# Output projection in eight pieces on the key tiles, MLP operands in pairs, chunk one split early: a two-layer fp32 encoder step on one core

## The reference, cut to what matters

```python
x = x + o.reshape(bsz, t, H * 64) @ w_o          # output projection, 1024 x 1024
x = x + sq_relu_mlp(rmsnorm(x, norm_ffn[l]), w_up[l], w_down[l])   # 1024 -> 4096 -> 1024

def sq_relu_mlp(h, w_up, w_down):
    return jnp.square(jax.nn.relu(h @ w_up)) @ w_down
```

## Time and profile before

| | us |
|---|---|
| median of three runs | 1664.33 (1663.49 to 1667.38) |
| the profiled execution's own time | 1654.25 |
| its span, first to last instruction | 1652.4 |
| PE busy | 1533.6 |
| DVE busy | 1108.5 |
| ACT busy | 728.2 |
| POOL busy | 431.2 |
| mean granted TensorE clock, share of full | 0.970 |

### The profile page before, as it was taken

How to read it: one execution, slowest core, us unless ns; L and a number is a source line. 1 busy time by engine, 2 the same in 40 slices (tenths; PEclk the granted TensorE clock), 3 DMA queues, 4 the chain that set the end, 5 groups by cost and what they waited for, 6 DMA issues and landing times.

```text
span 1652.4 us, 30854 instructions
## 1 busy us (share of the span) xinstructions
PE 1533.6 (93%) x10826; PEld 1445.4 (87%) x10826; DVE 1108.5 (67%) x1970; ACT 728.2 (44%) x1500; POOL 431.2 (26%) x441
## 2 busy tenths in 40 slices
PE   4999979998979999999999897999897999999997
PEld 3787759997969999999988686998886999999997
DVE  4132037775788788788765236778478888888875
ACT  3313137774444433333334434777444334333424
POOL 1110034552342122122100003455243221222210
PEclk8999969999989999999999998999999999999999
DMA  7245331211021221331240537221022123312211
GB/s 261 87 141 159 125 98 49 58 40 52 26 77 52 102 102 51 102 102 51 76 144 11 180 135 220 65 64 33 1 77 77 63 90 102 102 53 99 102 51 58
DMA packets 119316, 146.06 MB, mean 88 GB/s; under 512 B 17632, under 2 KB 95520, under 8 KB 119248
## 3 DMA queue, kind: packets, MB, share of 16 engines
q1 hardware_dynamic: 119248, 145.16, 26.9%
HBM read 120.54 MB, written 24.60 MB: 88 GB/s over the span
## 4 chain that ended last, share of the span: by engine, by line
PE 80%; issue 6%; DVE 5%; ACT 4%; DMA 2%; POOL 1%; SPq 1%; POOLq 0%; DVEq 0%; ACTq 0%
PE ps L1663 47%; PE ps L1990 19%; PE ps L1825 3%; PE ps L1869 2%; PE ps L1870 2%; PE ps L1871 2%; ACT wh L861 1%; DVE wl L1204 1%; PE ps L1840 1%; PE ps L1796 1%; PE ps L1848 1%; POOL sacc L712 1%; PE ps L1818 1%; DVE wul L1406 0%; ACT wuh L1010 0%
## 5 line engine op out<-in xcount | busy, mean ns | idle before, releaser
L1496 DVE TENSOR_TENSOR xT<-xT,ps 128x592 f32<-128x592 f32 (+1 forms) x256 | 194.9, 762 | 51.3 <-PE ps L1663 49.0
L812 POOL TENSOR_TENSOR ssum<-raw 128x512 f32<-128x512 f32 x32 | 42.9, 1341 | 485.3 <-DVE wul L1406 482.2
L1990 PE MATMUL ps<-bh,wuh 128*128 128x296 f32 (+1 forms) x512 | 153.3, 299 | 11.3 <-issue 4.4
L744 POOL TENSOR_TENSOR prob<-prob,rs 128x144 f32<-128x144 f32 (+4 forms) x160 | 117.0, 745 | 140.4 <-DVE rs L1310 140.2
L1990 PE MATMUL ps<-bl,wuh 128*128 128x296 f32 (+1 forms) x512 | 153.2, 299 | 0.0
L1990 PE MATMUL ps<-bh,wul 128*128 128x296 f32 (+1 forms) x512 | 152.7, 298 | 0.0
L1320 DVE TENSOR_TENSOR ptl<-ps,pth 128x256 fp32r<-128x256 f32 (+2 forms) x192 | 95.9, 502 | 65.3 <-ACT pth L948 65.2
L1663 PE MATMUL ps<-wh,xgh 128*128 128x512 f32 (+5 forms) x320 | 122.8, 384 | 11.5 <-issue 4.3
L1990 PE MATMUL ps<-th,wuh 128*128 128x296 f32 (+1 forms) x384 | 116.2, 303 | 13.5 <-DVE snap L1476 11.0
L1663 PE MATMUL ps<-wl,xgh 128*128 128x512 f32 (+5 forms) x320 | 121.9, 381 | 0.0
L1663 PE MATMUL ps<-wh,xgl 128*128 128x512 f32 (+5 forms) x320 | 121.5, 380 | 0.0
(11 more groups left out here) (244 smaller groups left out, 4674.0 us busy)
## 6 DMA issues: line engine op xcount, KB each, us to landing
raw<-in_w_up SPq DMA_DIRECT2D x32, 1024.0 KB, 7.1
raw<-in_w_down SPq DMA_DIRECT2D x32, 1024.0 KB, 5.1
raw<-in_w_in_a SPq DMA_DIRECT2D x12, 1024.0 KB, 7.3
kv_mla<-stn SPq DMA_DIRECT2D x24, 256.0 KB, 2.4
raw<-in_w_o_a SPq DMA_DIRECT2D x4, 1024.0 KB, 7.2
natk<-kv_mla SPq DMA_DIRECT2D x8, 512.0 KB, 3.5
raw<-in_w_o_b SPq DMA_DIRECT2D x4, 1024.0 KB, 12.1
q_mla<-stn SPq DMA_DIRECT2D x16, 192.0 KB, 1.9
```

The source lines that it names most:

```text
L744: g.tensor_tensor(prob[0:rows, c, off:off + n], prob[0:rows, c, off:off + n], rs[0:rows, u:u + 1].to_broadcast([rows, n]), ALU.mult).then_ ...
L812: g.tensor_tensor(ssum[:, 1, :, :], a11, a21, ALU.subtract).then_inc(s_ready, 1)
L1496: v.tensor_tensor(a, a, two_banks(2 + m % 2, n), ALU.add).then_inc(x_ready if last else acc_done, 1)
L1990: i = te.matmul(ps[:, bank, 0:h], w[:, k, :], x, start=(u not in (3, 4, 6) and k == 0 and p == 0), stop=(k == 3 and p == 2), skip_group_ch ...
```

## The change

- w_o comes in eight pieces of 128 columns (0.5 MB each, 512-byte runs), all issued by `load_wo`, in layer 0 ahead of block 5's stores, in layer 1 where the four were. `wo_high` and `wo_low` split a piece into one of two places in turn, which are those of the keys (`kh`, `kl`) of the even and the odd heads. Piece 0 is split inside head 15's step, piece 1 behind the last turned group and ahead of `out(15)`, piece m+2 in step m of `operands`. To make that possible, `prob`, `kh`, `kl`, `qh`, `ql`, `pth` and `ptl` get new places, and the memsets of `prob` are ten for five.
- PE begins piece 0 between the last attention products: k-steps 0 and 1 ahead of head 15's first weighted product, 2 to 6 behind the last turn, and 7 behind `out(15)` (`wo_first`).
- MLP operands: B21 with B22 and T2 with T3 are made by one instruction each on ACT and DVE; the sign of B12 is turned with a negated gain (`gN`) so that T2 and T3 are one broadcast sum; T4 gets a place of its own.
- POOL's weight sums of chunk 0 stand one by one behind the sums of squares of steps 2 to 5, those of chunk 1 behind those of steps 6 and 7. Chunk 0's units are split in steps 2, 4, 5, 6 (three) and 7, where it was four in step 6 and three in 7.
- First period: ACT splits chunk 1's units 2 to 6 ahead of the inner squares; DVE splits units 2 and 3 between the combinations, takes the variance later, and copies the spread and does both norms behind the last combination.
- The raw slots of the MLP change (up 0 and 2, sums in 1, down 3), with the waits of the first loads; the load of q_down's first half no longer waits for the last down split.

```diff
-W_IN0, WO_A0 = 0, 12
-KVD0, QD0, KVU0, QU0, WO_B0, W_END = 16, 18, 20, 22, 26, 30
+KVD0, QD0, KVU0, QU0, W_END = 12, 14, 16, 18, 22
...
+        def wo_raw(m):
+            return raw[:, m // 2, 1024 * (m % 2):1024 * (m % 2) + 1024].rearrange("p (k c) -> p k c", c=P)
+        def wo_half(t, m):
+            return t[:, 4 + 2 * (m % 2):6 + 2 * (m % 2), :].rearrange("p u (k c) -> p (u k) c", c=P)
...
+            def load_wo(layer):
+                sp.wait_ge(lo_done, KVD0 if layer == 0 else W_END)
+                for m in range(KD):
+                    sp.dma_start(wo_raw(m), wo_src(layer, m)).then_inc(wo_in, 16)
...
             for b, (kind, hf) in enumerate(BLOCKS):
-                for j in (2 * b + 4, 2 * b + 5):
-                    load(j)
+                if b < 4:
+                    for j in (2 * b + 4, 2 * b + 5):
+                        load(j)
+                if b == 5:
+                    load_wo(0)
...
             load(KVD0 + 1)
+            load(QD0)
             sp.wait_ge(dl_done, 4 * NCH)
-            load(QD0)
...
+            def wo_high(layer, m):
+                act.wait_ge(wo_in, 128 * (layer + 1))
+                if m == 0:
+                    act.wait_ge(s_ps, 5 * (HEADS * layer + HEADS - 1))
+                elif m == 1:
+                    act.wait_ge(s_ps, 5 * HEADS * (layer + 1))
+                else:
+                    act.wait_ge(wo_ps, KD * layer + m - 1)
+                s.activation(wo_half(wuh, m), wo_raw(m), ACT.Copy).then_inc(wo_hi, 1)
...
                         exp(h, c, u)
+                        if last and u == 0:
+                            wo_high(layer, 0)
...
+                wo_high(layer, 1)
                 out(HEADS - 1, 1, PAIRS - 1)
...
+            def wo_low(layer, m):
+                dve.wait_ge(wo_in, 128 * (layer + 1))
+                dve.wait_ge(wo_hi, KD * layer + m + 1)
+                v.tensor_tensor(wo_half(wul, m), wo_raw(m), wo_half(wuh, m).bitcast(F32), ALU.subtract).then_inc(wo_lo, 1)
...
                     if not last:
                         qk(h, 2, 1 - c)
+                    else:
+                        wo_low(layer, 0)
                     row_max(h, 3)
...
+                    dve.wait_ge(wo_ps, KD * layer + m + 1)
                     a = halves(xT[:, m, 0:n])
                     v.tensor_tensor(a, a, two_banks(m % 2, n), ALU.add).then_inc(x_ready, 1)
+                    if m + 2 < KD:
+                        wo_low(layer, m + 2)
...
-                        scaled(t24[:, 0:h], m, second, t1f[:, k, 0:h], ALU.add)
-                        scaled(t3f[:, 0:h], m, second, b12[:, k, 0:h], ALU.subtract)
-                        lo_x("B21", k, m, first)
-                        lo_x("B22", k, m, second)
-                        lo_tmp("T2", k, t24[:, 0:h])
-                        scaled(t24[:, 0:h], m, first, t24[:, 0:h], ALU.subtract)
-                        lo_tmp("T3", k, t3f[:, 0:h])
-                        lo_tmp("T4", k, t24[:, 0:h])
+                        x22 = xT[:, m, second].unsqueeze(1).to_broadcast([P, 2, h])
+                        v.scalar_tensor_tensor(t23[:, :, 0:h], x22, gain_of(m), pre[k][:, :, 0:h],
+                                               ALU.mult, ALU.add).then_inc(op_tmp, 1)
+                        hi_ready("B21", k)
+                        v.scalar_tensor_tensor(operand_pair("B21", k, True, h), halves(xT[:, m, 0:2 * h]), gain_of(m),
+                                               operand_pair("B21", k, False, h).bitcast(F32), ALU.mult, ALU.subtract).then_inc(op_lo, 1)
+                        tmp_ready("T2", k)
+                        hi_ready("T2", k)
+                        v.tensor_tensor(operand_pair("T2", k, True, h), t23[:, :, 0:h],
+                                        operand_pair("T2", k, False, h).bitcast(F32), ALU.subtract).then_inc(op_lo, 1)
...
+                for m in range(KD):
+                    step(m, {2: (0,), 4: (1,), 5: (2,), 6: (3, 4, 5), 7: (6,)}.get(m, ()))
...
-                    if not down:
-                        variance(b - 1, 6)
                     dve.wait_ge(p_ps, c * 7 + (7 * c0 + 7 + 5))
                     combine(c, snap[:, 2, 0:h], 1, snap[:, 0, 0:h], ALU.add)
                     dve.wait_ge(u_add, c * 5 + (5 * c0 + 5 + 2))
                     combine(c, hu[:, 1, h:n], 2, snap[:, 2, 0:h], ALU.subtract)
+                    if not down:
+                        variance(b - 1, 6)
                     dve.wait_ge(p_ps, c * 7 + (7 * c0 + 7 + 6))
                     combine(c, hu[:, 1, 0:h], 3, snap[:, 2, 0:h], ALU.add)
+                    if down:
+                        norm(c + 1, 1)
+                    else:
+                        up_lo(layer, c + 2, par, 2, True)
+                    dve.wait_ge(p_ps, c * 7 + (7 * c0 + 7 + 7))
+                    combine(c, hu[:, 0, h:n], 2, snap[:, 1, 0:h], ALU.subtract)
                     if not down:
                         spread()
-                    norm(c + 1, 1)
-                    dve.wait_ge(p_ps, c * 7 + (7 * c0 + 7 + 7))
-                    combine(c, hu[:, 0, h:n], 2, snap[:, 1, 0:h], ALU.subtract)
+                        norm(c + 1, 1)
                     norm(c + 1, 0)
...
                     if k == 4:
+                        wo_first(0, 2)
                         weighted_v(HEADS - 1, 0, p_split(HEADS, 1) + G0, PAIRS - 1, 1, 1)
+                wo_first(2, PAIRS - 1)
                 for part in (1, 2, 3):
                     weighted_v(HEADS - 1, part, p_split(HEADS, 4 if part < 3 else 5) + G0, PAIRS - 1, 1, 1)
+                pe.wait_ge(o_lo, H0 + HEADS)
+                wo_first(PAIRS - 1, PAIRS).then_inc(wo_ps, 1)
```

More of the change, by code:

```diff
@@ L678, in _ @@
             mla_q(1, 1)
-            for j in range(WO_B0, W_END):
-                load(j)
+            load_wo(1)
             with sp.Fori(0, PAIRS // 2 - 1) as i:
@@ L1061, in mlp @@
+                    for u in units:
+                        up_hi(layer, 0, 0, u, True)
+                for m in range(KD):
+                    step(m, {2: (0,), 4: (1,), 5: (2,), 6: (3, 4, 5), 7: (6,)}.get(m, ()))
             def mlp(layer):
@@ L1092, in period @@
                     if more:
-                        for u in range(2, 4):
+                        for u in range(2, 4 if down else 7):
                             up_hi(layer, c + 2, par, u, not down)
@@ L1096, in period @@
                     inner(c + 1, 1 - par, 0)
-                    if more:
+                    if more and down:
                         for u in range(4, 7):
-                            up_hi(layer, c + 2, par, u, not down)
+                            up_hi(layer, c + 2, par, u)
                 period(-1, 1, down=False)
@@ L1470, in mlp @@
+                    for u in units:
+                        up_lo(layer, 0, 0, u, True)
+                for m in range(KD):
+                    step(m, {2: (0,), 4: (1,), 5: (2,), 6: (3, 4, 5), 7: (6,)}.get(m, ()))
             def mlp(layer, gain):
@@ L1535, in period @@
                     inner_lo(c + 1, 1 - par, 0)
-                    for m in range(2, KD):
+                    for m in range(2 if down else 4, KD):
                         if down:
```

355 lines of the change are left out of this document (173 added, 182 removed).

## The result

The changed kernel takes 1651.64 us (median of 6 runs, 1650.13 to 1654.57) against 1664.87 for the kernel before in the same session; the ratio is 0.9926, with a 95% interval of 0.9913 to 0.9940. That is 12 to 13 us faster, where 23 were forecast: the sign was right, the size was nearly twice what came.

A forecast was written before the change was run, and what follows sets the result against it. TensorE is busy for 93% of the span, so only its waits or lower clock can be won. Savings of 8.7 + 10.0 + 2.6 + 1.6 + 0.4 = 23.3 us from the median 1664.33 give 1641.0, range 1631 to 1652.

The forecast's parts named there:

- Start of the projection: Output projection, from its first possible product to its end: 58.0 us, 8.7 less, in layer 0; 10.0 less in layer 1.
- Splits in the ring: ACT and DVE steps beside PE's projection pieces: splitting piece m+2 is hidden if DVE is under 4 us late.
- operands in pairs: DVE's MLP operand steps m = 4 to 7: paired operations take 0.5 us less a step.
- Rival A: Steps 4 to 6: DVE operations behind squares meet POOL's sums, add 7 3 us later a layer; 1650.0 in all; chance 0.20.
- (B): Steps fit better: chunk 0's product 1 waits under 1 us, head 15 hides its splits; 1633.0 in all; chance 0.15.
- To the end of chunk 0: Layer 0, piece 7's end to the spread's end: 17.8 us, including 2.6 waiting at product 1 and 1.5 of slower clock.
- The lower clock: Behind the gap after attention, nine matmul pairs ran 0.20 us slower each, a cost of 1.8.
- Moving the spread: Behind chunk 0's last combine: removes 3.6 us of wait and slower clock, but no gain, as the same DVE chain decides later.
- The fifth product's wait: MLP chunk 1: DVE's chain ahead of it takes 14.4 us for 15.4; PE waits about 7 where it waited 5.00.
- q_down: Its load, moved ahead of SP's wait for the down splits, removes PE's wait of 0.40: 0.4 us less.
- DMA: w_o's eight transfers, 8192 packets at 30.6 ns each over 16 engines, take 15.7 us, hidden in both layers.
- Rival C: Small-run w_o loads delay q's stores in layer 0 and pair 2's loads in layer 1; 1675.0 at 85 ns; chance 0.07.

The follow-up runs named there:

- unpaired: Changed kernel with VectorE's three wide operations of 592 columns in steps 4 to 7 made as six of 296; 1649.43 us, ratio 0.9921 to the kernel before.
- both: Changed kernel with GpSimd's chunk-one sums behind the last squares and VectorE's order in steps 4 to 7 altered; 1646.06 us, ratio 0.9887 to the kernel before.
- snap first: Changed kernel with the combine that chunk one's fifth product waits for put ahead of the four down splits; 1642.31 us, ratio 0.9860 to the kernel before.
- after: The changed kernel itself, all parts of the change, against the kernel before; median 1651.64 us, ratio 0.9926; its profiled execution took 1654.03 us.
- first profile of before: Kernel before, unchanged, the profiled execution the prediction read; 1654.25 us at a mean granted clock of 0.970.
- second profile of before: Kernel before, no edit, profiled once more; 1662.05 us at a clock of 0.962.

## Why the prediction was right and wrong

**The step that failed** is the one from piece 7's end to chunk one's first product. The prediction had 17.8 us there in layer 0; it took 23.1, and 23.5 in layer 1. The part behind it, to chunk one's fifth product, came as forecast: 14.2 and 14.1 for 14.4. The two together are 5.1 and 5.9 over their forecasts of 32.2 and 31.7; these 11.0 are about what is missing from the 23.3. Of the 5.3 over 17.8 in layer 0, 1.15 is a longer wait for add 7 (3.75 for 2.6), 1.80 a wait that had no term, and 2.1 lower clock (3.6 for 1.5). The waits come again in every profile that leaves the ring and POOL's sums alone (3.74 to 3.79, and 1.29 to 2.13, in layer 0); the clock part differs between executions by about its own size (unpaired: 21.5 in both layers, with waits of the same sum).

**Start of the projection: right.** 58.0 and 56.7 were forecast, with 0.6 in each for a delay of head 15, which lies ahead of this stretch; without it 57.58 stands against 57.4 and 56.08 against 56.1. The wait for out(15) is 1.55 to the hundredth, no clock fell behind it in this execution (in layer 0 of both and of snap first it did, for 1.5 us), and pieces follow each other every 6.57 us for 6.55. That delay was too low: from the wait before the last head's last scores to the projection's start it is 7.96 for 6.77, 1.2 and not 0.6, in layer 0 (and 10.18 for 6.76 in layer 1, 2.2 of it lower clock: PE stands at 0.41 a matmul there for 0.28).

**Splits in the ring and operands in pairs: why add 7 was late.** I had add 7 start 23.0 us behind piece 4's end. It starts 24.2 behind it (adds 24.15 apart, 24.29 in layer 1). By step it is 8.46, 7.89 and 7.80 for 8.0, 8.0 and 7.0, so step 6 is the worst. Two terms were too good: the pairs save 0.22 a step, not 0.5, because I took eight durations of 0.47 where most of the operations start 0.44 and less apart; and DVE idles in each step for ACT, 0.52 ahead of the last operation where the step of before that I scaled had 0.21, and in step 4 another 0.45 ahead of the split. One term was too bad: the second operation beside POOL in steps 4 and 5 costs 0.5 and not 1.1. Rival A, POOL's block, was the right place to look (without the squares' 1.2 a step add 7 is on time in layer 0) and stood at 3 us a layer; what came over my sum is 1.2. Add 7 starts 4.7 behind piece 7, between the two bounds given as signs of (A) and (B).

**To the end of chunk 0: the wait that had no term.** I let product 1 (the second) wait 2.6, charged 1.5 for lower clock and took every other wait of before as gone. Measured are 3.75, then 1.80 more before the fourth product, and lower clock behind both: 33 matmuls started 0.25 apart in place of 0.14, 3.6. The 1.80 comes from the two sums for chunk one that the change puts ahead of the last squares; I read the move ("spread over steps 2 to 5") and priced it in steps 4 to 6 alone. Taking it back and mending the order returns the stretch to 32.98, 0.8 from my number.

**The lower clock: a second term that failed.** I credited 1.8 us a layer for the upper clock behind the attention. In the profile of after it came (2.1 and 2.7 less PE time than in the first profile of before, 3.0 and 2.7 less than in the second), and part of it stands behind the new waits in chunk 0 instead (2.0 and 3.5 more against the first, 0.7 and 3.5 against the second). Some stands where the prediction had only its delay of 0.6 and no term for the clock: the end of the last head, which now waits 1.3 for its last scores where it waited 1.0. In the nine profiles here with the early start, that part took 9.7 to 10.3 us at the lower clock in 9 of 18 layers and 7.9 to 8.3 in the other 9; in the two profiles of before it ran at the upper clock in all four. Over the whole run the clock is that of before: 0.959 to 0.963, with a median of 0.961 in both.

**Moving the spread: right**, no gain by itself. **The fifth product's wait**: 6.45 for 7 forecast; right in size, but I took DVE's work as what sets it, and it was its order. **q_down: not shown.** The 0.40 is not in the profile of after, but it is not in the second profile of before either, so the 0.4 credited to the moved load can't be told from the difference between two executions. **DMA: right.** In the ten microseconds from 190 the queue of after shows

```profile
q1 hardware_dynamic: 5697, 2.88, 112.3%
```

which is 1.123 x 160 / 5697 = 31.5 ns a packet for the 30.6 taken; attention starts 1.9 later than before, but its wait for the keys is 8.4 for 8.5, so that is PE's own lateness from earlier stages. Eight pieces at 31.5 ns are 16.1 us for the 15.7 of the sum and the estimate of 25.7 beside rival C (eight times 3.2 is 25.6). Rival C fails.

**The sum.** In layer 0 the forecast has waits of 1.55 + 2.6 + 7 = 11.2 us where 8.59 + 12.27 = 20.9 stood, 9.7 less. Measured, from the turns of the last head on, are 2.39 + 12.64 = 15.0, 5.8 less; in layer 1 it is 1.8 + 13.4 for 9.47 + 12.61, 6.9 less. That is 12.7 us of waits in two layers, and the 3.6 of clock gave nothing over the whole run: 12 to 13 in the runs.

## What to carry to other kernels

When a change makes a DMA or a split vanish from the critical engine's waits, sum the next engine's step with its idle slots and its blocked operations, by starts and not by durations, and compare it with the critical engine's step: here steps of 7.8 to 8.5 us beside pieces of 6.57 left 4.5 us of backlog after three. Look for the short operation that the critical engine needs and that stands behind long ones nobody waits for yet (here 0.45 us behind four splits; moving it ahead of them took 5.6 us off PE's wait in each layer). And take a second profile before believing that two profiled executions compare: PE's busy time in the two of one kernel differed by 10.3 us, where the change was worth 12 to 13. Idle time, span less busy, differed by 2.5 and is the better thing to compare.

## What the runs showed that I had not expected

- Two profiles of one kernel were 7.8 us apart (1652.4 and 1660.2), of which PE's busy time was 10.3 and its waits -2.5.
- Closing DVE's waits for ACT, 0.97 us in step 4 and 0.52 in steps 5 and 6, won 1.25 of the 2.0: the operation that moved forward into POOL's window took 2.04 for 0.78.
- The lower clock does not follow from the waits alone: in after, with waits of 1.3 and up to 0.7 us, the last head ran at the upper clock in layer 0 (0.28 a matmul) and mostly at the lower in layer 1 (0.41). Over the nine profiles with the early start it is 9 of 18 layers. What decides it is not shown by these runs.
